# One diffusion step of an mLSTM and retention backbone on one core: the second down part opens with one whole tile, the transposes move inside a gate tile, and the rotary partner rows change queue

## The reference, cut to what matters

```python
def trunk(x, cond, grid, ...):
    for i in range(DEPTH):                                  # 2 layers
        sh1, sc1, g1, sh2, sc2, g2 = modulation(cond, ada_w[i], ada_b[i])
        u = rmsnorm(x, norm_gain[i, 0]) * (1 + sc1) + sh1
        y = mlstm_mixer(u, ...) if i == 0 else retention_mixer(u, ...)
        x = x + g1 * rmsnorm(y, norm_gain[i, 1])
        u = rmsnorm(x, norm_gain[i, 2]) * (1 + sc2) + sh2
        f = conv_ffn(u, ...)
        x = x + g2 * rmsnorm(f, norm_gain[i, 3])

def rot(xp, pos):                                           # rotary positions of q and k, layer 1
    x1, x2 = xp[..., :quarter], xp[..., quarter:]
    return jnp.concatenate([x1 * cos - x2 * sin, x1 * sin + x2 * cos], axis=-1)

# the end of each mixer: a norm per head, then the gate, then the output projection
h = head_norm((h_f + flip_t(h_b)).transpose(0, 2, 1, 3), g_norm).reshape(B, T, hv)
return (h * jax.nn.silu(gate)).astype(u.dtype) @ w_out, ...

# conv_ffn, with D_FF = 2816
h = dwconv3(u @ w_up, conv_w, conv_b)
g, up = jnp.split(h, 2, axis=-1)
return (jax.nn.gelu(g, approximate=True) * up) @ w_down
```

## Time and profile before

| | |
|---|---|
| median of 3 runs | 2033.01 us (2031.89 to 2033.78) |
| the profiled execution | 2038.16 us, its span 2036.3 us |
| PE matmul busy | 1939.3 us, 95% of the span |
| PE weight load busy | 1822.5 us, 89% |
| DVE busy | 1030.5 us, 51% |
| ACT busy | 700.1 us, 34% |
| POOL busy | 218.9 us, 11% |

### The profile page before, as it was taken

The page is one execution under the profiler, slowest core; times in us unless marked ns, Lnnn a source line. Parts: engine busy times, 40 slices in busy tenths (PEclk is TensorE's granted clock), DMA queues, the critical chain, the costliest instruction groups (busy, mean ns, idle before and its releaser), DMA issues.

```text
span 2036.3 us, 31430 instructions
## 1 busy us (share of the span) xinstructions
PE 1939.3 (95%) x12793; PEld 1822.5 (89%) x12793; DVE 1030.5 (51%) x1807; ACT 700.1 (34%) x903; POOL 218.9 (11%) x174
## 2 busy tenths in 40 slices
PE   7989999989999999999999999998999999999998
PEld 5668987759999999888999999997898999999997
DVE  4315435475653556458443343346377664455645
ACT  4324233344432333334322222224354332233333
POOL 3101001410000000141000000011240000000032
PEclk8989999999999999999999999999999999999999
DMA  9841302662223222244232221425742212323143
GB/s 284 306 163 40 106 27 73 243 223 63 66 60 88 75 82 69 80 125 160 75 98 64 93 72 36 129 73 172 242 124 63 83 48 76 104 62 82 55 131 114
DMA packets 273997, 220.44 MB, mean 108 GB/s; under 512 B 7995, under 2 KB 263731, under 8 KB 268275
## 3 DMA queue, kind: packets, MB, share of 16 engines
q1 hardware_dynamic: 262387, 196.33, 31.9%
q10 hardware_dynamic: 9808, 14.94, 2.5%
q0 software_dynamic: 1712, 7.88, 1.1%
HBM read 203.92 MB, written 11.01 MB: 106 GB/s over the span
## 4 chain that ended last, share of the span: by engine, by line
PE 82%; DVE 9%; ACT 3%; issue 2%; DMA 2%; POOL 1%; ACTq 1%; SPq 0%; DVEq 0%; POOLq 0%
PE PJ L1906 49%; PE PJ L1917 11%; PE PJ L2063 7%; PE AT L1885 1%; PE AT L2234 1%; DVE uT L1229 1%; PE AT L2218 1%; DMA hT<-in_ada_w 1%; DVE w_low L1292 1%; PE PJ L1927 1%; PE AT L1927 1%; PE AT L2231 1%; ACTq L923 1%; DVE diag L1216 1%; DVE xT L1225 1%
## 5 line engine op out<-in xcount | busy, mean ns | idle before, releaser
L1906 PE MATMUL PJ<-h_both,w_high 128*128 128x320 f32 x3872 | 736.9, 312 | 7.5 <-DVE sq L1705 4.6
L1906 PEld LDWEIGHTS PJ<-h_both,w_high 128*128 128x128 f32 x3872 | 614.3, 190 | 11.3 <-issue 10.2
L1705 DVE SCALAR_TENSOR_TENSOR sq<-PJ,cols,sq 128x127 f32<-128x127 f32 x516 | 193.7, 431 | 250.8 <-ACT sq L1112 238.3
L1906 PE MATMUL PJ<-h_both,w_low 128*128 128x320 f32 x1312 | 300.0, 310 | 0.0
L762 ACT ACTIVATE w_high<-ring 128x2048 fp32r<-128x2048 f32 (+1 forms) x92 | 163.6, 1778 | 177.6 <-PE PJ L1906 103.2
L1906 PEld LDWEIGHTS PJ<-h_both,w_low 128*128 128x128 f32 x1312 | 220.4, 189 | 0.0
L1292 DVE TENSOR_TENSOR w_low<-ring,w_high 128x2048 fp32r<-128x2048 f32 (+1 forms) x92 | 196.1, 2132 | 44.5 <-ACT w_high L762 44.5
L552 POOL TENSOR_TENSOR sqsum<-sqsum,sq 128x320 f32<-128x320 f32 x56 | 109.4, 1954 | 994.0 <-issue 824.3
L2063 PE MATMUL PJ<-w_high,h_both 128*128 128x256 f32 x960 | 178.3, 286 | 7.2 <-ACT xT L930 7.2
L2063 PEld LDWEIGHTS PJ<-w_high,h_both 128*128 128x128 f32 x960 | 151.9, 193 | 16.6 <-issue 8.6
L1906 PE MATMUL PJ<-h_both,ring_low 128*128 128x320 f32 x624 | 144.2, 313 | 0.0
(11 more groups left out here) (278 smaller groups left out, 2913.9 us busy)
## 6 DMA issues: line engine op xcount, KB each, us to landing
ring<-in_ffn_w_up SPq DMA_DIRECT2D x88, 512.0 KB, 5.0
hT<-in_ada_w SPq DMA_DIRECT2D x30, 1024.0 KB, 4.9
ring<-in_ffn_w_down SPq DMA_DIRECT2D x64, 384.0 KB, 4.1
ring<-in_ret_w_in SPq DMA_DIRECT2D x24, 1024.0 KB, 6.3
ring<-in_ret_w_out SPq DMA_DIRECT2D x14, 1024.0 KB, 5.6
ring<-in_ml_w_in SPq DMA_DIRECT2D x12, 1024.0 KB, 9.8
turn<-in_ada_w SPq DMA_DIRECT2D x10, 1024.0 KB, 7.5
ring<-in_ffn_w_down SPq DMA_DIRECT2D x32, 320.0 KB, 3.6
```

Of the source, the lines that this page charges most:

```text
L1705: ins = v.scalar_tensor_tensor(o, z, scalar, o, ALU.mult, ALU.add)
L1906: ins = pe.matmul(PJ[:, s, b, 0:HALF], w[:, at + k * step:at + k * step + P], x[:, k, b * HALF:(b + 1) * HALF], start=(k == 0 and n == 0), ...
```

## The change

Four edits:

1. **Second down part** (both layers). Output tile 0 is made whole, for both halves, with its 12 k tiles in two loads of 6: units n = 0 and 1. Then follow 7 half tiles for half 0 (n = 2 to 8) and 7 for half 1 (n = 9 to 15). The number of matmuls is the same, 576; there is one weight unit less of full size. The whole tile lies in PJ slot 1; slot 0 is passed over, and DVE raises its semaphore behind a memset of one number. DVE and the square on ACT read the whole tile at n = 1. The steps of the norms begin at n = 8 and there are 8 of them in place of 9.
2. **Turning back** (both layers, hh = 0). PE makes 6 of the 8 k tiles of gate tile 2, then transposes, then makes the last 2. On DVE the cast of the weight unit moves behind `hT`.
3. **Partner rows** (layer 1). SP issues the four DMAs, after the v loads and ahead of the gate loads, when both PJ slots have been read out. ACT doesn't issue or wait for them any more.
4. **Gap 1.** The squares of the last two x tiles are not added by POOL; PE sums them with two more matmuls in `x_stat_first`, which now stands at k = 5 of tile 13 instead of k = 2.

```diff
@@ norm tables
         ADD_AT = (((), (0, 1), (2, 3, 4), (5, 6, 7), (), (), ()),
-                  ((0,), (1, 2), (3, 4), (5, 6, 7), (), (), (), (), ()),
+                  ((0,), (1, 2), (3, 4), (5, 6, 7), (), (), (), ()),
...
-        SPLIT_AT = ((0, 0, 0, 0, 0, 0, 4, 16), (0, 0, 0, 0, 0, 0, 3, 7, 10, 16), (0, 0, 0, 0, 3, 7, 11, 16, 16, 16))
+        SPLIT_AT = ((0, 0, 0, 0, 0, 0, 4, 16), (0, 0, 0, 0, 0, 3, 7, 10, 16), (0, 0, 0, 0, 3, 7, 11, 16, 16, 16))
+        DOWN_STEP = HALVES[1] // 2
+        def down_at(n):
+            return (n - 1, 0) if n <= KT else (n - KT, 1)
+        def x_sums_to(gap):
+            return KT * gap - (2 if gap > 1 else 0)
@@ SP, layer 1
-                    with loop(sp, GROUPS[layer] - 1, **per(4, 4, CH, CH)) as g:
-                        load_v(g)
-                        load_gates(g)
-                        load_qk(g + 1)
+                    def swap():
+                        for s in range(2):
+                            sp.wait_ge(pj_free[s], evacs.now())
+                        evacs.add(9)
+                        for q in range(4):
+                            sp.dma_start(swapped[32 * q:32 * q + 32, :, :],
+                                         qk[32 * (q ^ 1):32 * (q ^ 1) + 32, :, PROMPT:TOK]).then_inc(swap_in, 16)
+                    load_v(0)
+                    sp.wait_ge(led_out, 2)
+                    swap()
+                    load_gates(0)
+                    load_qk(1)
+                    with loop(sp, GROUPS[layer] - 2, ev=(evacs, 9), **per(4, 4, CH, CH)) as g:
+                        load_v(g + 1)
+                        swap()
+                        load_gates(g + 1)
+                        load_qk(g + 2)
                     load_v(GROUPS[layer] - 1)
+                    swap()
                     load_gates(GROUPS[layer] - 1)
@@ ACT, evac_qkv
-                    if layer == 1:
-                        a.wait_ge(pj_free[0], free[0].now())
-                        a.wait_ge(pj_free[1], free[1].now())
-                        for q in range(4):
-                            a.dma_start(swapped[32 * q:32 * q + 32, :, :],
-                                        qk[32 * (q ^ 1):32 * (q ^ 1) + 32, :, PROMPT:TOK]).then_inc(swap_in, 16)
                     high_unit(3, 1)
@@ DVE, head_tail
                     ins.then_inc(hn_ready, 1)
-                    if split_next is not None:
+                    if split_next is not None and hh == 1:
                         low_unit(split_next)
...
                     ins.then_inc(h_ready, 1)
+                    if split_next is not None and hh == 0:
+                        low_unit(split_next)
@@ DVE, second down part
+                            s = pj(0)
+                            v.memset(wait_here[:, :], 0.0).then_inc(pj_free[s], 1)
+                            low_weights(0, DOWN_WIDE)
+                            for n in range(1, DOWN_HALF):
...
+                                if n == 1:
+                                    y, banks = uT[:, 0, :].rearrange("p (b t) -> p b t", b=2), PJ[:, s, :, 0:HALF]
+                                else:
+                                    m, b = down_at(n)
...
+                                v.tensor_tensor(y, banks, y, ALU.add).then_inc(pj_free[s], 1)
@@ PE, statistics
             def x_stat_first(gap):
-                pe.wait_ge(sqx_added, KT * (gap + 1))
-                pe.matmul(mean_half[0], mean_w, sum_half[:, 0, :], start=True, stop=True).then_inc(stat_full, 1)
+                pe.wait_ge(sqx_added, x_sums_to(gap + 1))
+                ins = pe.matmul(mean_half[0], mean_w, sum_half[:, 0, :], start=True, stop=(gap != 1))
+                if gap == 1:
+                    for k in range(KT - 2, KT):
+                        pe.wait_ge(sqx_ready, 2 * KT * gap + k + 1)
+                        ins = pe.matmul(mean_half[0], mean_w, sq_x[:, k % 2, :], start=False, stop=(k == KT - 1))
+                ins.then_inc(stat_full, 1)
@@ PE, gate tile 2 of both mixers
+                def turn_in_gate():
+                    split_unit(1)
+                    s = pj_slot()
+                    project_piece(s, 0, range(0, KT - 2), 1)
+                    turn_back()
+                    project_piece(s, 0, range(KT - 2, KT), 1)
...
                             if hh == 0:
-                                gate(2)
+                                turn_in_gate()
...
-                            turn_back()
+                            if hh == 1:
+                                turn_back()
@@ PE, second down part
-                        first_slots = []
-                        for ks in (range(HALVES[1] - 1), range(HALVES[1] - 1, HALVES[1])):
-                            for t in range(2):
...
+                        free[pjn.n % 2].add()
+                        pjn.add()
+                        whole = pj_slot()
+                        for n in range(2):
+                            pe.wait_ge(l_split[n], splits[n].add())
+                            for k in range(n * DOWN_STEP, (n + 1) * DOWN_STEP):
+                                pe.wait_ge(act_ready, FT * layer + first + k + 1)
...
+                            ins.then_inc(made[n], 1)
```

More of the change, by code:

```diff
@@ L514, in _ @@
                     start = kind == "up" and first == 0
[L515 to L519 removed]
+                    if kind == "down" and first > 0:
+                        for s in range(2):
+                            sp.wait_ge(l_split[s], splits[s].add())
+                            load_down(s, 0, first + s * DOWN_STEP, DOWN_STEP // 2, down)
+                        for again in range(2):
+                            if again:
+                                for s in range(2):
+                                    sp.wait_ge(l_split[s], splits[s].add())
+                                    load_ffn(kind, layer, s, (KT - 1, 1)[s], first, up, down)
+                            with loop(sp, KT // 2 - 1, sp0=(splits[0], 1), sp1=(splits[1], 1)) as i:
+                                for s in range(2):
+                                    sp.wait_ge(l_split[s], splits[s].add())
+                                    load_ffn(kind, layer, s, i * 2 + (s + 1 + again), first, up, down)
+                        continue
+                    with loop(sp, turns - start, sp0=(splits[0], 1), sp1=(splits[1], 1)) as i:
+                        for s in range(2):
+                            sp.wait_ge(l_split[s], splits[s].add())
+                            load_ffn(kind, layer, s, i * 2 + (s + 2 * start), first, up, down)
                 for s in range(2):
@@ L556, in add_x @@
                 pool.wait_ge(sqx_ready, 2 * KT * gap + k + 1)
-                done = KT * gap + k
+                done = x_sums_to(gap) + k
                 if done > 0:
@@ L2355, in _ @@
-                        for t in range(2, DOWN_HALF):
-                            j, b = t % 2, t // KT
+                        free[pjn.n % 2].add()
[5 more added lines that the diff above has]
+                                pe.wait_ge(act_ready, FT * layer + first + k + 1)
+                                at = (k - n * DOWN_STEP) * P
+                                for i, (w, x) in enumerate(((w_high, act_high), (w_high, act_low), (w_low, act_high))):
+                                    for b in range(2):
+                                        ins = pe.matmul(PJ[:, whole, b, 0:HALF], w[n][:, at:at + P],
+                                                        x[:, k, b * HALF:(b + 1) * HALF],
+                                                        start=(k == 0 and i == 0), stop=(k == HALVES[1] - 1 and i == 2))
+                            ins.then_inc(made[n], 1)
@@ L2357, in _ @@
+                        for n in range(2, DOWN_HALF):
+                            j, b = n % 2, down_at(n)[1]
                             pe.wait_ge(l_split[j], splits[j].add())
                             def before(k):
-                                if t == KT and k == 6:
+                                if n == KT + 1 and k == 6:
                                     y_stat(gap, 0)
-                                if gap < 3 and t == KT + 5 and k == 2:
+                                if gap < 3 and n == KT + 5 and k == 5:
```

96 lines of the change are left out of this document (47 added, 49 removed), and 2 rows, old and new, of the table ADD_AT.

## The result

The changed kernel takes 2007.13 us in the median of 4 runs (2005.79 to 2007.82), the kernel before 2032.45 (2030.86 to 2033.78). The ratio is 0.9874, with a 95% interval of 0.9854 to 0.9894: 25.3 us less. In two later groups of runs the same pair gave 0.9865 (0.9851 to 0.9880) and 0.986 (0.9843 to 0.9877), that is 28.2 and 28.9 us. The direction and the size of the forecast (25.9 us) stood; what the experiments changed is which places the gain comes from.

A forecast was written before the change was run, and what follows sets the result against it. TensorE holds 82% of the chain, so time is won only where PE waits or runs slowly. 9.8 + 3.0 + 7.2 + 6.2 - 0.3 = 25.9 us, from 2033.0 to 2007.1 us; range 2000 to 2014.5.

The forecast's parts named there:

- turn back: Inside gate tile 2, earlier transposes shorten PE's wait for hT: 6.4 us in layer 1, 3.4 in layer 0, 9.8 taken.
- partner rows: Layer 1: issued by SP, they free ACT, so the v projections' four waits for its readout go: 7.2 us.
- clock in layer 0: Behind the shortened hT waits the granted clock stays up: 1.5 us for each of two gate tiles, 3.0 together.
- second down parts: Both layers: two weight waits give way to one opening wait of 3.7 us; 3.1 us gained per layer, 6.2 together.
- gap 1: Lead pair starts 5.4 us sooner against 5.28 less covering work; counted as 0.3 us lost.
- first stretch: Layer 0, 3.9 us at clock 0.60 right behind the hT wait: held by the next head's exponentials, its 1.6 not counted.
- upper bound of 4.6: Second down part, gain in us for each layer if no clock drop follows the opening wait.
- lower bound of 1.5: Second down part, gain in us for each layer if a second clock drop occurs.
- a rival asked what if it were not there: Second down part: slot 1 is read out before PE arrives, no opening wait; 6.8 us more gained, 2000.3 us; chance 0.07.
- the root: Gap 1: ACT's square root in the norm starts 3.7 us sooner, after PE waits some 2.5 us for the last square.
- The gate weights: Layer 1, behind the partner rows on SP: landed at 1097.5, nothing lost; rival that they come late has chance 0.12.

The follow-up runs named there:

- turn_late_l0: Changed kernel with, in layer 0 alone, transposes behind gate tile 2 again and the weight cast ahead of hT; 2014.99 us, ratio 0.9912 to the kernel before.
- squares_by_pool: Changed kernel, but POOL adds all eight x squares of gap 1 and PE makes no extra statistics matmuls; 2007.82 us, ratio 0.9856 to the kernel before.

## Why the prediction was right, step by step

| term | forecast | from the stretches |
|---|---|---|
| turn back, both layers, and partner rows | 9.8 + 7.2 = 17.0 | 3.3 + 13.5 to 14.4 = 16.8 to 17.7 |
| clock in layer 0 | 3.0 | 3.05 to 4.5 |
| second down parts | 6.2 | 5.1 to 7.8 |
| gap 1 | -0.3 | 0.9 to 1.2 |
| sum | 25.9 | 25.9 to 31.2 |

The medians say 25.3 to 28.9.

**Turning back.** Right. The later turn back in layer 0 is worth 83.22 - 81.56 = 1.66 us, and the first one 1.67 (from DVE's copy of that head's state, `Cout`, to its `hT`: 23.73 before and 22.06 after), 3.3 in both, against the forecast of 3.4. In layer 1 it is 1.55 in each of four groups, 6.2 against 6.4.

**Partner rows.** Right in mechanism, a little short in size. The summed stretches give 13.5 to 14.4 for both edits of layer 1, against 6.4 + 7.2 = 13.6. Less the 6.2 of turning back, 7.3 to 8.2 are left for the partner rows, where the rows of waits have 6.3 and 7.2 us. So each of the four waits costs some 0.2 us more than its row says: a matmul's record is 0.31 us long at a pitch of 0.147, and the idle time is counted from its end.

**The clock in layer 0.** The sum was right, the places were not. I left out the first stretch of 1.6 us because the exponentials would hold it, and counted 1.5 for each of two gate tiles. Against the kernel before both stretches of the first head are won in full (3.05 us), and the third head's tile only against the first profile of before (1.43). The reason for leaving out the first stretch was wrong: it was the clock that held it and not the exponentials, since its eight matmuls took 2.4 us at the higher level in `turn_late_l0`. That run also shows that the 1.6 us of this stretch do not hang on the edit alone, since they didn't come back with it; the 1.4 of each tile did, 2.8 in both. Why the drop in the kernel before began earlier is open. That the sum of 3.0 was met is in part luck.

**The second down part.** Right: the new wait was forecast as 3.7 and is 3.65, layer 0 gained 58.6 - 55.5 = 3.1 in two of three profiles. The upper bound of 4.6 came up in the one part without a drop of the clock, and 2.0 to 2.3, not quite the lower bound of 1.5, in two with a longer one. The step with which the prediction passed by 8.7 us was this same wait: it was priced, and a rival asked what if it were not there, but not whether slot 0 would avoid it.

**Gap 1.** The sign was wrong, the step is the root. Its start was put 3.7 us sooner, and it is 31.13 - 26.75 = 4.4 sooner: PE waits for POOL's last addition, and that for 1.85 us, not 2.5 for the square. DVE's chain behind it is 1.8 us shorter, as said, and the reciprocal of half 1 cost nothing: 6.2 against 5.28. But `squares_by_pool` shows that a later root costs only half of its delay (0.7 of 1.3 us), so the path through the root, by which the prediction summed this term, is not the only one that binds.

**The gate weights.** The median of the weight loads put their landing at 1097.5; measured, on the time axis of before (the first partner row is issued at 1086.82 there and at 1067.44 after, 19.4 apart), it is 1078.7 + 19.4 = 1098.1, and that cost nothing, since the cast starts at 1081.34 + 19.4 = 1100.7. The Trainium skill, page "DMA: Bandwidth & Descriptors", section "Queues, rings and completion order", says that each DMA engine consumes the descriptors of a ring in order, and from this the prediction made 1103.5. The traces agree with the order: in all four groups the rows and then the gate weights land as they were issued. What failed is the step from the order to the time. The prediction set a whole landing of 6.3 us behind the last row's, but the first gate load landed only 2.7 to 3.7 us behind it, and the last row was there at 1076.0 + 19.4 = 1095.4 and not at 1097.2. Behind the rows a load takes 2 us longer than by itself, and not 6. No run here shows what the two transfers share.

**What stays open.** The single edits undone cost 11.5, 13.0 and 10.7 us and some 4 for the down parts, 39 in sum, while all together are worth 28. The traces show where most of the excess is: in layer 1, in drops of the clock that neither the kernel before nor the changed one has (3 and 2 places, 1.6 us each), and in `turn_late_l0` in 5.3 us outside the edited stretches, mostly in places where other kernels' profiles lose the same without that edit. Why a wait of 2 us is followed by the lower clock at one place and not at another was not settled, nor what gave the first head of layer 0 its longer drop in both profiles of before.

## What to carry to other kernels

Price a wait between matmuls twice: its idle time plus 0.2 us, and a possible drop of the clock behind it, 1.4 to 1.6 us here. The second can't be read off the length of the wait: behind 1.5 us the clock never fell (0 of 4), behind 3.65 mostly (16 of 18), and behind about 2 us it fell at some places and never at others. When a tile is moved to the front of a stage, look at who last held each of the two accumulator slots, since the one that alternation gives may be the one read out last. A single edit undone doesn't measure that edit's share where a clock is involved. Compare fixed stretches of several profiles, and before you charge a loss to an edit, look whether kernels without it lose the same there.

## What the runs showed of the hardware

- The same wait of 2.1 us for `hT` in the same code had no lower clock behind it in 8 of 8 cases in the kernel before, and one behind 3 of 4 (a granted 0.59 over 4.2 us where a window was read) in the changed kernel with only this wait put back. I had expected the place itself to decide.
- The same wait of 1.87 us behind the first head of layer 0 had the lower clock start within its first eight matmuls in both profiles of before (0.60 over 3.9 us in the first), and only behind them in `turn_late_l0` (1.00 over 2.4 us, then 0.81 over 8.8).
- Four DMAs of 256 KB between places in the core's own memory landed after 7.3 us in the median when ACT issued them just behind a weight load of 1 MB on SP, and after 4.2 when SP issued them in front. A pair of weight loads of 1 MB each took 5.3 and 7.6 us by itself and 7.4 and 9.4 directly behind the four.
- Issuing the four DMAs took SP 3.22 us where it had taken ACT 4.42.
